# A decode state update whose two matmuls per step read partitions 0 to 31 and 32 to 63 instead of 0 to 31 twice

## The reference, cut to what is computed

```python
m_new = m_t[..., -1]
w_end = jnp.exp(b[..., -1:] - b + igc - m_new[..., None])
decay = jnp.exp(b[..., -1] + m - m_new)
C_new = decay[..., None, None] * C + jnp.einsum('bhs,bhsk,bhsv->bhkv', w_end, kc, vc)
n_new = decay[..., None] * n + jnp.einsum('bhs,bhsk->bhk', w_end, kc)
```

## Time and profile before

| | |
|---|---|
| time, three runs | 2919.41, 2920.44, 2926.59 us; median 2920.44 us |
| the profiled execution | 2920.05 us, its span 2918.2 us |
| PE busy | 2782.0 us (95% of the span) |
| PE weight loads busy | 1971.6 us (68%) |
| DVE, ACT, POOL busy | 1252.5, 585.5, 417.2 us (43%, 20%, 14%) |
| mean DMA rate | 117 GB/s |
| mean granted TensorE clock | 0.978 |

### The profile page before, as it was taken

How to read it: one execution, slowest core, us unless ns; L and a number is a source line. 1 busy time by engine, 2 the same in 40 slices (tenths; PEclk the granted TensorE clock), 3 DMA queues, 4 the chain that set the end, 5 groups by cost and what they waited for, 6 DMA issues and landing times. The chain is left out here.

```text
span 2918.2 us, 39863 instructions
## 1 busy us (share of the span) xinstructions
PE 2782.0 (95%) x15729; PEld 1971.6 (68%) x15729; DVE 1252.5 (43%) x2165; ACT 585.5 (20%) x1367; POOL 417.2 (14%) x819
## 2 busy tenths in 40 slices
PE   8987999999999999999999999999699999699998
PEld 6663458874864488888888888888555564455553
DVE  3142398667755644232222144441322330345453
ACT  3122458643000000000000100100232231111211
POOL 0000014211000000000000022220133100333341
PEclk9998989999999999999999999999999999699999
DMA  6447202122122312312332354452945214665652
GB/s 232 99 136 221 111 19 65 47 69 84 48 82 80 105 44 72 80 60 80 110 116 69 104 156 139 137 159 81 317 148 151 80 41 134 202 199 161 202 164 77
DMA packets 275029, 341.52 MB, mean 117 GB/s; under 512 B 44972, under 2 KB 228004, under 8 KB 269564
## 3 DMA queue, kind: packets, MB, share of 16 engines
q1 hardware_dynamic: 237836, 259.50, 28.5%
q0 software_dynamic: 16288, 67.46, 7.6%
q10 hardware_dynamic: 20720, 12.01, 1.4%
HBM read 261.44 MB, written 80.01 MB: 117 GB/s over the span
## 5 line engine op out<-in xcount | busy, mean ns | idle before, releaser
L1346 PE MATMUL sbank<-w,xT 128*128 128x256 f32 x3328 | 732.1, 381 | 5.9 <-issue 3.0
L1346 PEld LDWEIGHTS sbank<-w,xT 128*128 128x128 f32 x3328 | 630.7, 190 | 95.3 <-issue 4.6
L1346 PE MATMUL sbank<-w,area 128*128 128x256 f32 x1664 | 361.3, 379 | 0.0
L1737 DVE TENSOR_TENSOR pout_b<-pout_b,sbank 128x256 f32<-128x256 f32 x320 | 134.3, 421 | 512.4 <-PE sbank L1346 415.3
L1346 PEld LDWEIGHTS sbank<-w,area 128*128 128x128 f32 x1664 | 315.9, 190 | 42.8
L1695 DVE TENSOR_TENSOR w<-w 128x2048 f32<-128x2048 f32 x64 | 145.1, 2288 | 345.1 <-PE sbank L1346 281.1
L2040 PE MATMUL at_bank_bc<-w,at_hT 128*128 128x512 f32 x512 | 230.0, 593 | 3.9 <-ACT at_bc_out L2195 3.9
L1421 ACT ACTIVATE pout_b<-sbank 128x256 f32<-128x256 f32 x128 | 48.4, 383 | 900.0 <-PE sbank L1346 656.8
L1346 PE MATMUL sbank<-w 128*128 128x256 f32 x832 | 181.7, 379 | 0.0
L1346 PEld LDWEIGHTS sbank<-w 128*128 128x128 f32 x832 | 158.1, 190 | 21.5
L1343 PE MATMUL sbank<-xT,w 128*128 128x512 f32 x384 | 167.4, 594 | 0.0
(11 more groups left out here) (437 smaller groups left out, 3362.0 us busy)
## 6 DMA issues: line engine op xcount, KB each, us to landing
w<-in_w_in SPq DMA_DIRECT2D x64, 1024.0 KB, 5.3
proj<-pout_b SPq DMA_DIRECT2D x208, 128.0 KB, 1.7
area<-in_x_prompt SPq DMA_DIRECT2D x16, 1024.0 KB, 7.4
attention_then_units<-proj SPq DMA_DIRECT2D x128, 128.0 KB, 2.5
area<-roped_q_of_decode POOLq DMA_DIRECT2D x32, 256.0 KB, 4.0
w<-in_w_out SPq DMA_DIRECT2D x4, 2048.0 KB, 15.7
y_of_groups_b_c<-at_bc_out SPq DMA_DIRECT2D x32, 256.0 KB, 2.3
out_sample_C<-mo_dec_states SPq DMA_DIRECT2D x32, 256.0 KB, 2.8
```

The source lines that it names most:

```text
L1346: last = nc.tensor.matmul(bank[t][:, 0:256], x(c, t * P, (t + 1) * P), at[name][:, c, :], start=first_ and c == 0, stop=c == 7, skip_group ...
L1737: nc.vector.tensor_tensor(out[:, t, :], x[:, t, :], product_at(n, t), ALU.add).then_inc(sums_read, 1)
```

## The change

The keys and the values of the 32 decode rows are laid out on 64 partitions. Partitions 0 to 31 hold columns 0 to 127 of each head's keys, partitions 32 to 63 columns 128 to 255; the values stand twice, on both. The first matmul of a decode step reads partitions 0 to 31, the second 32 to 63. For this

- SP loads the second half of each head's keys a second time, to partitions 32 to 63 (one more transfer);
- ACT loads `dec_row_of` and the decode values twice (two more transfers), so `mlstm_consts` is awaited at 112, not 96;
- the 12 gate columns of the decode rows are turned a second time, to PSUM partitions 32 to 63 (one more small matmul on PE), and ACT and DVE copy and scale 64 partitions instead of 32;
- POOL's `dec_kw` and `dec_k_slot` work on 64 partitions x 128 columns instead of 32 x 256;
- L3116 and L3091 read the values on partitions 0 to 31, as before.

```diff
+                    sp.dma_start(k.area[NS:2 * NS, 8192 + ML_W:8192 + 2 * ML_W].rearrange("t (h c n) -> t h c n", h=ML_H, c=2)[:, :, 0, :],
+                                 k.proj[SEQ:TOK, C_K:C_K + ML_W].rearrange("t (h c n) -> t h c n", h=ML_H, c=2)[:, :, 1, :]
+                                 ).then_inc(k.dqk_in, 16)
...
-        dq1, dk1 = T("dec_q_slot", [P, 2, ML_H, 2, NS]), T("dec_k_slot", [NS, 2, ML_D])
-        dv, dkw = T("dec_v", [NS, ML_H, V1]), T("dec_kw", [NS, ML_W])
+        dq1, dk1 = T("dec_q_slot", [P, 2, ML_H, 2, NS]), T("dec_k_slot", [2 * NS, 2, P])
+        dv, dkw = T("dec_v", [2 * NS, ML_H, V1]), T("dec_kw", [2 * NS, ML_H, P])
...
+        dk_of = xin[0:2 * NS, ML_W:2 * ML_W].rearrange("p (h c n) -> p h c n", h=ML_H, c=2)
...
-            act.dma_start(drow[:, :], ins["dec_row_of"][:, :]).then_inc(consts_in, 16)
-            act.dma_start(dv[:, :, 0:ML_D], k.proj[SEQ:TOK, C_V:C_V + ML_W].rearrange("t (h d) -> t h d", h=ML_H)
-                         ).then_inc(dv_in, 16)
+            for x in range(2):
+                act.dma_start(drow[NS * x:NS * (x + 1), :], ins["dec_row_of"][:, :]).then_inc(consts_in, 16)
+                act.dma_start(dv[NS * x:NS * (x + 1), :, 0:ML_D],
+                             k.proj[SEQ:TOK, C_V:C_V + ML_W].rearrange("t (h d) -> t h d", h=ML_H)).then_inc(dv_in, 16)
...
                     for h in range(ML_H):
-                        nc.gpsimd.tensor_scalar(dkw[:, h * ML_D:(h + 1) * ML_D], dk[:, h * ML_D:(h + 1) * ML_D],
-                                                cols[0:NS, NCH, 2, h:h + 1], None, ALU.mult).then_inc(d_kw, 1)
+                        nc.gpsimd.tensor_scalar(dkw[:, h, :], dk_of[:, h, 0, :], cols[0:2 * NS, NCH, 2, h:h + 1], None,
+                                                ALU.mult).then_inc(d_kw, 1)
...
-                    nc.gpsimd.tensor_tensor(dk1[:, m % 2, :], dkw[:, h * ML_D:(h + 1) * ML_D],
-                                            drow[:, b:b + 1].to_broadcast([NS, ML_D]), ALU.mult).then_inc(k_slot, 1)
+                    nc.gpsimd.tensor_tensor(dk1[:, m % 2, :], dkw[:, h, :], drow[:, b:b + 1].to_broadcast([2 * NS, P]),
+                                            ALU.mult).then_inc(k_slot, 1)
...
                 for c in range(2):
-                    last = nc.tensor.matmul(kv[c][:, 0:V1], dk1[:, u, c * P:(c + 1) * P], dv[:, h, :], start=True,
-                                            stop=True)
+                    half = slice(NS * c, NS * (c + 1))
+                    last = nc.tensor.matmul(kv[c][:, 0:V1], dk1[half, u, :], dv[half, h, :], start=True, stop=True)
                 last.then_inc(d_kv, 1)
...
+            last = nc.tensor.matmul(acc1[NS:2 * NS, 12 * NCH:12 * NCH + 12], r12[:, SEQ:TOK], k.ident[0:12, 0:12],
+                                    start=True, stop=True)
```

More of the change, by code:

```diff
@@ L2474, in mix_out @@
         ds, rowd = T("dec_states", [P, 8, 2, V1]), T("dec_rows_everywhere", [P, 2, ML_H, NS])
-        dmask, drow = T("dec_mask", [NS, NS]), T("dec_row_of", [NS, DEC_B])
+        dmask, drow = T("dec_mask", [NS, NS]), T("dec_row_of", [2 * NS, DEC_B])
         dqT, dkT = T("dec_qT", [P, 8, NS]), T("dec_kT", [P, 8, NS])
-        dq1, dk1 = T("dec_q_slot", [P, 2, ML_H, 2, NS]), T("dec_k_slot", [NS, 2, ML_D])
-        dv, dkw = T("dec_v", [NS, ML_H, V1]), T("dec_kw", [NS, ML_W])
+        dq1, dk1 = T("dec_q_slot", [P, 2, ML_H, 2, NS]), T("dec_k_slot", [2 * NS, 2, P])
+        dv, dkw = T("dec_v", [2 * NS, ML_H, V1]), T("dec_kw", [2 * NS, ML_H, P])
         dee, ddt, dsd = (T(n, [NS, P]) for n in ("dec_ee", "dec_dt", "dec_sd"))
         dq, dk = xin[0:NS, 0:ML_W], xin[0:NS, ML_W:2 * ML_W]
+        dk_of = xin[0:2 * NS, ML_W:2 * ML_W].rearrange("p (h c n) -> p h c n", h=ML_H, c=2)
         do, dz, dgain = T("dec_o", [P, ML_D]), T("dec_z", [P, ML_D]), T("dec_gain", [P, ML_D])
@@ L2680, in _ @@
             dve.wait_ge(cols_kept, 2)
-            for x in (cols[:, 0:NCH, 2, :], cols[0:NS, NCH, 2, :]):
+            for x in (cols[:, 0:NCH, 2, :], cols[0:2 * NS, NCH, 2, :]):
                 nc.vector.tensor_scalar(x, x, K_SCALE, None, ALU.mult).then_inc(cols_kept, 1)
@@ L2687, in _ @@
                 nc.vector.tensor_copy(x[:].rearrange("p c n -> p (c n)"), y_[:, 0:8 * NS]).then_inc(d_kept, 1)
-            dve.wait_ge(consts_in, 96)
+            dve.wait_ge(consts_in, 112)
             for s in slots:
@@ L2819, in _ @@
                                  ).then_inc(cols_kept, 1)
-            nc.scalar.activation(cols[0:NS, NCH].rearrange("p a h -> p (a h)"), acc1[0:NS, 12 * NCH:12 * (NCH + 1)],
-                                 ACT.Copy).then_inc(cols_kept, 1)
+            nc.scalar.activation(cols[0:2 * NS, NCH].rearrange("p a h -> p (a h)"),
+                                 acc1[0:2 * NS, 12 * NCH:12 * (NCH + 1)], ACT.Copy).then_inc(cols_kept, 1)
             act.wait_ge(cols_kept, 2)
@@ L2905, in out_root @@
                                         ).then_inc(o_rooted, 1)
-            pool.wait_ge(consts_in, 96)
+            pool.wait_ge(consts_in, 112)
             for s in slots:
@@ L2923, in _ @@
                     pool.wait_ge(cols_kept, 4)
-                    pool.wait_ge(d_in, 32)
+                    pool.wait_ge(d_in, 48)
                     for h in range(ML_H):
-                        nc.gpsimd.tensor_scalar(dkw[:, h * ML_D:(h + 1) * ML_D], dk[:, h * ML_D:(h + 1) * ML_D],
-                                                cols[0:NS, NCH, 2, h:h + 1], None, ALU.mult).then_inc(d_kw, 1)
+                        nc.gpsimd.tensor_scalar(dkw[:, h, :], dk_of[:, h, 0, :], cols[0:2 * NS, NCH, 2, h:h + 1], None,
+                                                ALU.mult).then_inc(d_kw, 1)
                 if s == -1:
@@ L3066, in _ @@
                     last.then_inc(n_turned, 1)
-                    pe.wait_ge(d_in, 32)
+                    pe.wait_ge(d_in, 48)
                     for x, bank in ((dq, kv0), (dk, kv1)):
@@ L3090, in _ @@
                     for h in range(ML_H):
-                        last = nc.tensor.matmul(dnum[NS * h:NS * (h + 1), 0:V1], zero[:, :], dv[:, h, :], start=False,
+                        last = nc.tensor.matmul(dnum[NS * h:NS * (h + 1), 0:V1], zero[:, :], dv[0:NS, h, :], start=False,
                                                 stop=True, skip_group_check=True)
@@ L3113, in _ @@
                     pe.wait_ge(d_sd, 1)
-                    pe.wait_ge(dv_in, 16)
+                    pe.wait_ge(dv_in, 32)
                     for h in range(ML_H):
-                        nc.tensor.matmul(dnum[NS * h:NS * (h + 1), 0:V1], dsd[:, h * NS:(h + 1) * NS], dv[:, h, :],
+                        nc.tensor.matmul(dnum[NS * h:NS * (h + 1), 0:V1], dsd[:, h * NS:(h + 1) * NS], dv[0:NS, h, :],
                                          start=True, stop=False, skip_group_check=True)
```

## The result

| | before | changed |
|---|---|---|
| time, median of 6 runs each on the same chip | 2923.52 us (2919.41 to 2930.16) | 2905.99 us (2901.08 to 2909.31) |
| ratio, 95% interval | | 0.9937 [0.9922, 0.9952] |
| the profiled execution, its span | 2920.05, 2918.2 us | 2909.31, 2907.5 us |
| PE, DVE, POOL busy | 2782.0, 1252.5, 417.2 us | 2771.1, 1255.0, 410.2 us |

The ratio is a gain of 18.4 us (14 to 23), the two medians lie 17.5 us apart; forecast were 14.8 us and 2905.3 us. Two more groups of runs of the same changed kernel, on other chips, gave 0.9934 [0.9909, 0.996] and 0.993 [0.9913, 0.9946].

What follows compares the result with a forecast made beforehand. PE was taken to bound the kernel from slot 5 on; savings of 11.8 (steps 4 to 31), 2.5 (steps 1 to 3) and 0.5 us (start) sum to 14.8, from 2920.05 to 2905.3 us, range 2902.5 to 2912.5.

Steps and rivals of the forecast that it cites:

- Two rounds instead of four: Decode step at full clock: products on other rows and banks run in pairs, saving 0.42 us per step.
- three rounds: Rival, decode step: one product's two pairs keep order; 0.21 us saved per step, 2912.4 us; chance 0.05.
- no overlap: Rival, decode step: 32-row products on other rows still queue, only the start gains; 2919.5 us; chance 0.08.
- each change of rows costs a drain: Rival, decode step: changing rows costs 0.20 us like a change of shape; 2940.0 us, slower; chance 0.04.
- Steps 4 to 31: Decode steps at full clock where PE never waits: 28 x 0.42 = 11.8 us saved.
- Nothing late next: From slot 5 on: no other engine becomes late; DVE's idle time in its fullest slot falls 2.09 to 1.67 us.
- Steps 1 to 3 at half clock: Early slots: each step lies on the chain though PE idles; 3 x 0.83 = 2.5 us saved.
- The start: Start of `mix_out`: later constants +0.9 us, narrower `dec_kw` -1.4 us; sum -0.5 us, between -1.5 and +1.4.
- the clock's part: Steps 1 to 3: another granted clock could lose the 2.5 us and 1.7 us more, or gain 1.7 us.
- The sum: Whole kernel: 11.8 + 2.5 + 0.5 = 14.8 us saved, 2905.3 us.
- the case's range: Whole kernel: the forecast's own bounds, 2902.5 to 2909.5 us, without the rivals.

Runs made afterwards that it cites:

- e1: Changed kernel with both products of a decode step reading partitions 0 to 31 again; median 2918.06 us, ratio 0.9983 to before.
- e2: Changed kernel with only the first of the two products of each decode step; median 2900.56 us, ratio 0.9931.
- e8: The kernel before, unedited, profiled once more; 2924.75 us in one run.
- e5: Changed kernel with unused identity products as filler where PE idles in slots 0 to 4; median 2907.46 us, ratio 0.9951.
- e11: e10 with unused identity products in slots 0, 3 and 4, none at slot 2; 2900.3 us, ratio 0.9929.
- e6: e5 with both products of a decode step on partitions 0 to 31; 2917.1 us, ratio 0.9984.
- e3: Changed kernel with an already satisfied semaphore wait of PE between the two products of a step; 2910.11 us in one run.
- e4: Changed kernel with the late output weights issued by SP at the stage's start, not from POOL's queue; median 2907.19 us, ratio 0.9951.
- e10: e4 with the first decode states issued right behind ACT's constants; median 2905.62 us, ratio 0.9941.

## Why the prediction was right, and where it was off

- **Two rounds instead of four, 0.42 us a step.** Shown, at 0.43 (1.06 to 0.63). L1257 was the right row to reason from, though it has 64 rows and not 32. e1 gives the 0.43 us back when only the row numbers are restored, and e2 shows that the second product is hidden whole. The rivals "three rounds" (a step of 0.85 us), "no overlap" (1.06) and "each change of rows costs a drain" (over 1.06) are out with that one number. The Trainium skill's "TensorE: Matmul & The Clock Gate", section "Part 3: Packing small matmuls", would have had the three rounds, if its program order held for the two pairs of one float32 product. The trace disagrees with that reading: in each of the two rounds of the changed step two matmuls start within 0.01 us.
- **Steps 4 to 31, 11.8 us.** Measured 307.99 (mean of two profiles) less 295.98, and 0.46 us in what follows the start of step 31 (54.12 to 53.66): 12.5 us. By the first profile of before alone, the one that the sum was made against, it is 12.2 us. Of that the rows give 12.0, 28 x 0.43, as e1 shows, and 0.2 is the wait for `mo_a` in the earlier trace rows, which is gone in e1 too. The mean of two has 0.3 us more by e8's one late load.
- **Nothing late next.** Held: one wait of PE in 350 us. DVE's idle time fell by 0.21 us and not by 0.42; I had taken the whole saving from that one wait, and 0.21 us of it came off the other, behind POOL's statistics (1.55 to 1.34 us). The loads have less room than DVE: e2, e5 and e11, and of the kernel before e8, have one or two slots 0.5 to 0.7 us longer, in which PE waits 0.3 to 0.5 us for a unit's load. None of the three unedited profiles of the changed kernel has such a wait.
- **Steps 1 to 3 at half clock, 2.5 us.** The size of a step is shown: 2.01 to 1.15 us, where 0.83 less was forecast. That the step lies on the chain is shown for one of the three slots, at full clock (7.11 to 6.68 us, e6 and e5). What the three were worth together isn't: the means of the profiles fall from 29.2 us (two) to 26.0 us (three), 3.2 us, in a stretch that varies by 6 us with the clock, and the pair at nearly the same clock says 1.2 us.
- **The start, -0.5 us.** Its path was right, its parts came nearly as put, and together they came to nothing. `dec_kw` takes 0.59 us each (2.36 us for four below) where 0.55 was taken. Timeline of ACT's issues and of POOL in the changed kernel, beside the earlier trace rows:

```profile
2496.93 0.45 ACTq L2819 DMA_DIRECT2D mo_dec_row_of<-in_dec_row_of  x1
2497.41 0.45 ACTq L2820 DMA_DIRECT2D mo_dec_v<-proj  x1
...
2501.44 1.10 POOL L2876 TENSOR_TENSOR mo_ee<-attention_then_units,mo_causal 128x128 f32<-128x128 f32 x2 [215.16 <-DMA mo_dec_row_of<-in_dec_row_of]
...
2503.36 2.36 POOL L2931 TENSOR_SCALAR mo_dec_kw<-area,mo_cols 64x128 f32<-64x128 f32 x4
```

  From the stage's start POOL begins at 9.66 us (2501.44 - 2491.78), where before had 8.66 (2495.53 - 2486.87). By more profiles: 8.66 and 9.26 us before, 9.05 to 11.45 in six with the new layout (the changed kernel, e1, e2, e3), 1.2 us later on the mean, where 0.9 was taken; and `dec_kw` gives 1.28 us back, where 1.4 was taken. In these eight profiles PE leaves its wait for the load at slot 2 from 22.0 to 22.3 us after POOL issues the late output weights, while that issue itself moves from 14.6 to 17.0 us. So the start does work through POOL's queue, as forecast. The issue comes at 15.4 and 16.0 us before, at 15.7 us on the mean of the six: the term is 0.0 and not -0.5, and it moves by 2.4 us from run to run.

  The sum left out that DVE is slowed. Its four products for `dec_qT`, which the change leaves as they are, come while POOL is in `dec_kw` before, and mostly behind it now, beside other work of POOL. Before, and the changed kernel:

```profile
2499.50 0.72 DVE L2701 TENSOR_TENSOR mo_dec_qT<-mo_dec_qT,mo_dec_rows_everywhere 128x64 f32<-128x64 f32 x4
```

```profile
2505.30 3.34 DVE L2705 TENSOR_TENSOR mo_dec_qT<-mo_dec_qT,mo_dec_rows_everywhere 128x64 f32<-128x64 f32 x4
```

  They take 0.72 us in both profiles of before and 3.3 us or more in all with the new layout, and step 0 starts at 26.6 us or later and not at 25.4 or 25.7. In e4, e10 and e11 SP issues the weights and they are still slow, so POOL's issue of them isn't needed for it; what slows them isn't shown. In the changed kernel the path doesn't see it, since PE waits for the load behind step 0 anyway (5.94 us at slot 2).
- **What e1 adds.** e1, which has this layout and not the rows, is 5.0 us faster than before by its ratio (2 to 8). The start doesn't explain that. In its one profile the stage is 5.3 us shorter than the mean of before's two (425.7, 431.05): 1.9 us by step 1, of which 1.0 by a load that lands early (the weights' issue before it is at 14.6 us, the earliest of the eight), 3.0 us more by step 4 and 0.5 after it, with 10.2 us at half clock where before has 16.3 and 19.4. All but the last 0.5 lies in stretches in which the unedited changed kernel varies by as much. Whether the layout brings less time at the lower clock or that run was merely lucky stays open, as e1's ten runs have one profile. I had put the clock's part at up to 1.7 us either way, and the three profiles of the changed kernel alone show 6.
- **The sum.** By the profiles the stage became 15.8 us shorter (431.05 to 415.3, means of two and three), by the runs the program 18.4 us; forecast were 14.8. The 15.8 are 0.1 us up to step 1, 3.2 from step 1 to 4 and 12.5 after it. Only the last stands clear of how much one kernel varies from run to run; that the sum comes as near as it does is in part luck. The number fell within the range, but of the 15 runs of the changed kernel 7 lie below its lower end, 2902.5 us: there was too little for the early slots' clock. At the other end my own bounds add up to more than the case's range says: 11.8 - 1.7 - 1.4 = 8.7 us saved is 2911.3 us and not 2909.5.
- **A change of rows costs nothing, a change of shape does.** Inside the step nothing is added: the product on other rows starts 0.01 us after the first. At its ends the pace breaks. The changed kernel, single matmuls before the step and in the next group:

```profile
2657.34 0.38 PE L3017 MATMUL mo_bank_turn_h<-ident_sb,mo_a 128*128 128x128 f32 x2
...
2657.45 0.27 PE L3017 MATMUL mo_bank_turn_h<-ident_sb,mo_a 128*128 128x128 f32 x1
...
2658.81 0.59 PE L3032 MATMUL mo_bank_acc<-area,w 128*128 128x512 f32 x1
```

  The last of L3017 starts at 2657.45 us, 0.11 after the one before it, and the step 0.20 us after that: 0.09 over the pace. The step's second round starts 0.32 us after its first, 0.11 over the 0.215 of a round. On the way out it is the same once more: 0.31 us to the next group, 0.09 over, and 0.53 us from that group's first matmul (2658.28) to its second, 0.10 over the 0.43 of 512 columns. So each of the two changes of shape costs 0.20 us, 0.4 us a step, and the step's 0.63 us hold half of each. The forecast counted only that half. Groups of the same full shape follow each other at their own pace (0.43 us from the last 128x512 matmul to L2981). "TensorEngine Tiling (Array Packing)" of the Trainium skill, section "Tiling Modes", key properties, says that a change of mode drains the engine and a change of tile doesn't; the trace agrees that the one costs time and the other none, and doesn't show that a drain is the reason.

**Not tried:** four products on four row groups (two decode steps at once). It would need four PSUM banks in place of two, and these are shared with `key_values`. The 0.4 us that the changes of shape cost around each step could be shared that way; no run here shows it.

## What to carry to other kernels

Where PE is the bound and a product has few rows, look whether its neighbour can read other partitions and write another bank: with both, the second cost nothing here (0.63 us for one or two). The partitions are what e1 shows to matter; the bank was another before as well, and one bank for both wasn't run. Price it from a place in the same trace where such products already alternate, count what a change of shape costs at both ends apart (0.4 us around each step here), since it stays, and ask whether the next engine has more slack than you save. Then measure against a control that has the new layout and the old rows: without e1 the 2 to 8 us that are there without them would have been put down to the rows, or the match of forecast and result taken for a proof of each term. And profile a kernel more than once before a term of a few microseconds is read off a stretch in which PE idles.

## What the runs showed of the hardware that I had not expected

- The same program, unedited, takes 22.6 to 28.5 us for the same three sparse slots, with 6.7 to 17.8 us of them at the lower clock, and repeats to 0.01 us in the 296 us that follow, where PE never pauses. Where a unit's load came late there, the cost was 0.5 to 0.7 us a time (e8, e2, e5, e11).
- Four short products of DVE, 128 x 64 each, took 0.72 us before and 3.34 us in the changed kernel, without a change to them. Both times POOL was at work beside them; what slowed them isn't shown.
- On POOL a product of 64 x 128 takes two thirds of the time of one of 32 x 256, not half; its group in the changed kernel, busy us and mean ns, beside 648 ns in the earlier trace rows:

```profile
L2946 POOL TENSOR_TENSOR mo_dec_k_slot<-mo_dec_kw,mo_dec_row_of 64x128 f32<-64x128 f32 x27 | 11.8, 435 | 0.0
```
